# Routing tokens to experts: a row-count sort on chip and narrow column pieces in four pairs, in place of a fixed pairing with an overflow pair

## What is computed

```python
def hierarchical_moe(h, w_rg, b_rg, w_re, b_re, w_gate, w_up, w_down):
    ...
    pg = jax.nn.softmax(g_logits, axis=-1)
    pg_top, g_idx = lax.top_k(pg, 1)
    ...
    pe_top, j_idx = lax.top_k(pe, TOP_K)
    weights = pg_top * pe_top / jnp.sum(pe_top, axis=-1, keepdims=True)
    e_idx = g_idx * EXPERTS_PER_GROUP + j_idx
    combine = jnp.sum(jax.nn.one_hot(e_idx, N_EXPERTS, dtype=jnp.float32) * weights[..., None], axis=1)
    ...
    for e in range(N_EXPERTS):
        act = jax.nn.silu(hf @ w_gate[e]) * (hf @ w_up[e])
        y = y + combine[:, e:e + 1] * (act @ w_down[e])
    return y.reshape(b_, s_, d_)
```

## Time and profile before

| | us |
|---|---|
| three runs | 1675.55, 1676.64, 1677.65 (median 1676.64) |
| the profiled execution, its time | 1675.31 |
| the profiled execution, its span | 1673.4 |
| TensorE busy over the span | 1571.5 |
| VectorE busy | 825.1 |
| ScalarE busy | 543.1 |
| GpSimd busy | 84.3 |

### The profile page before, as it was taken

The page is one execution under the profiler, slowest core; times in us unless marked ns, Lnnn a source line. Parts: engine busy times, 40 slices in busy tenths (PEclk is TensorE's granted clock), DMA queues, the critical chain, the costliest instruction groups (busy, mean ns, idle before and its releaser), DMA issues.

```text
span 1673.4 us, 19707 instructions
## 1 busy us (share of the span) xinstructions
PE 1571.5 (94%) x8009; PEld 1183.4 (71%) x8009; DVE 825.1 (49%) x1442; ACT 543.1 (32%) x881; POOL 84.3 (5%) x106
## 2 busy tenths in 40 slices
PE   7999999999999999999999899999999996888875
PEld 7987777777787788888887688787678883333322
DVE  6546334355355776666323884437663736222211
ACT  5334444354433322222113433342354323111110
POOL 5000000000000000000000010000000001121110
PEclk9999999999999999999999999999999996989998
DMA  5334212122233455565222232221214467999995
GB/s 164 116 101 128 76 51 76 51 76 76 69 95 114 151 183 190 186 221 176 101 101 89 60 103 87 89 66 62 76 51 151 159 231 303 382 414 403 402 407 188
DMA packets 147070, 260.41 MB, mean 156 GB/s; under 512 B 16568, under 2 KB 121316, under 8 KB 133664
## 3 DMA queue, kind: packets, MB, share of 16 engines
q1 hardware_dynamic: 138544, 241.41, 41.1%
q0 software_dynamic: 8432, 17.70, 3.6%
HBM read 253.79 MB, written 15.25 MB: 161 GB/s over the span
## 4 chain that ended last, share of the span: by engine, by line
PE 83%; DVE 7%; issue 4%; ACT 3%; DMA 2%; POOL 0%; POOLq 0%; DVEq 0%; ACTq 0%
PE psum L2498 20%; PE psum L2499 20%; PE psum L2500 20%; PE psum L3079 7%; PE psum L3096 4%; PE psum L2809 1%; PE psum L2798 1%; PE psum L2781 1%; PE psum L3057 1%; DVE cst L2012 1%; DVE WL L1560 1%; DMA Xg<-h_rows,tok 1%; PE psum L2703 1%; ACT Sb L1114 1%; DMA h_rows<-h2t 1%
## 5 line engine op out<-in xcount | busy, mean ns | idle before, releaser
L1560 DVE TENSOR_TENSOR WL<-raw,WH 128x2048 fp32r<-128x2048 f32 (+1 forms) x100 | 226.6, 2266 | 177.1 <-ACT WH L1029 176.8
L2498 PE MATMUL psum<-AHs,WH 128*128 128x512 f32 x744 | 305.9, 411 | 7.5 <-DVE WL L1560 4.6
L2500 PE MATMUL psum<-AHs,WL 128*128 128x512 f32 x744 | 292.6, 393 | 0.0
L2499 PE MATMUL psum<-ALs,WH 128*128 128x512 f32 x744 | 292.1, 393 | 0.0
L1029 ACT ACTIVATE WH<-raw 128x2048 fp32r<-128x2048 f32 (+1 forms) x100 | 189.0, 1890 | 129.1 <-PE psum L2500 97.7
L2498 PEld LDWEIGHTS psum<-AHs,WH 128*128 128x128 f32 x744 | 141.4, 190 | 44.3 <-DVE ALs L1748 5.8
L2498 PE MATMUL psum<-AH,WH 128*128 128x512 f32 (+1 forms) x464 | 169.2, 365 | 0.0
L2499 PE MATMUL psum<-AL,WH 128*128 128x512 f32 (+1 forms) x464 | 164.0, 353 | 0.0
L2499 PEld LDWEIGHTS psum<-ALs,WH 128*128 128x128 f32 x744 | 141.6, 190 | 30.9 <-issue 3.1
L2500 PE MATMUL psum<-AH,WL 128*128 128x512 f32 (+1 forms) x464 | 163.2, 352 | 0.0
L2500 PEld LDWEIGHTS psum<-AHs,WL 128*128 128x128 f32 x744 | 140.9, 189 | 30.7
(11 more groups left out here) (561 smaller groups left out, 2277.4 us busy)
## 6 DMA issues: line engine op xcount, KB each, us to landing
raw<-w_in SPq DMA_DIRECT2D x45, 1024.0 KB, 5.2
WE<-w_gate SPq DMA_DIRECT2D x34, 1024.0 KB, 19.3
WE<-w_up SPq DMA_DIRECT2D x34, 1024.0 KB, 23.1
WE<-w_down SPq DMA_DIRECT2D x34, 1024.0 KB, 19.0
araw<-w_ada SPq DMA_DIRECT2D x24, 1024.0 KB, 5.6
raw<-w_ffn_in SPq DMA_DIRECT2D x22, 1024.0 KB, 7.9
...
```

What stands on the lines that cost most here:

```text
L1560: V.tensor_tensor(WL[:, n, 0:w], raw[:, n, 0:w], WH[:, fed[0] % HL, 0:w].bitcast(F32), ALU.subtract).then_inc(S_("lo_ready"), 1)
L2498: MM(dst, lh, rh, start=first, stop=False)
L2499: MM(dst, lh, rl, start=False, stop=False)
L2500: return MM(dst, ll, rh, start=False, stop=last)
```

## The change

Three experts of each half of the list (13 to 15 and 29 to 31) stay at fixed pairs 0 to 2 (`HELD` = 3), since their weights are loaded before the counts are known. The other 13 of each half are sorted by row count on chip, the first half falling and the second half rising, and fill pairs 3 to 15. Each half of a pair takes 64 rows except in four pairs: in pairs 3 and 4 the first expert has 96 rows and the second 32, in pairs 14 and 15 it is the reverse. A half of 96 rows is worked as a product of 64 and one of 32 stationary columns (`parts_of`), so such a pair issues three products where others issue two. `OVER` is gone, `BASE` is 16; the branch runs if any expert has more rows than its place. SyncE reads both expert numbers of each pair from a list `order` (made by `sorted_places` on VectorE) ahead of its loads. `widths` and `rows_and_pairs` are the rest of the index work on VectorE, which moves behind pair 0's row and gate steps; y_scaled(0) moves behind gated(1).

```diff
-BASE = NE // 2 + 1
-NPAIR = BASE + NOV - 2
-
-OVER = 3
+BASE = NE // 2
+NPAIR = BASE + NOV
+
+HELD = 3
+SORTED = NE // 2 - HELD
+WIDE = 2
...
+        def held(t, half):
+            return NE // 2 * half + SORTED + t
+
+        def parts_of(t):
+
+            if t >= BASE:
+                return [(0, CAP, 0)]
+            if HELD <= t < HELD + WIDE:
+                return [(0, 64, 0), (64, 96, 0), (96, 128, 1)]
+            if t >= BASE - WIDE:
+                return [(0, 32, 0), (32, 64, 1), (64, 128, 1)]
+            return [(0, 64, 0), (64, 128, 1)]
 
         choice_gap, choice_exp, weight1, weight2 = (r4[:, n, :] for n in (0, 1, 2, 3))
 
         def more_tiles(eng):
 
             eng.wait_ge(*when("overflow_ready", 1))
-            return eng.value_load(eover[0:1, NOV:NOV + 1], min_val=0, max_val=NOV) > 2
+            return eng.value_load(eover[0:1, NOV:NOV + 1], min_val=0, max_val=NOV) > 0
 
 
         @block.sync
...
+            load_gate(sp, 2, 1, held(2, 1), 0)
             sp.wait_ge(*when("dense_ready", len(GROUPS)))
-            load_expert(sp, 1, 1, 1)
-            load_gate(sp, 2, 0, 2, 0)
+            load_expert(sp, 1, 1, held(1, 1))
+            load_gate(sp, 2, 0, held(2, 0), 0)
             sp.wait_ge(*when("h2_stored", 16 * NB))
-            load_gate(sp, 2, 1, NE // 2 + 2, 1)
-            sp.wait_ge(*when("overflow_ready", 1))
-            over = [sp.value_load(eover[0:1, x:x + 1], min_val=0, max_val=NE - 1) for x in range(2)]
+            load_gate(sp, 2, 1, held(2, 1), 1)
+            sp.wait_ge(*when("order_ready", 1))
             sp.wait_ge(*when("out_set", 16 * 3))
-            load_pair(sp, OVER, over)
-            for t in range(OVER + 1, BASE):
-                x = t - 1
-                load_pair(sp, t, (x + NE // 2, x) if x % 2 else (x, x + NE // 2))
+            for t in range(HELD, BASE):
+                load_pair(sp, t, [sp.value_load(order[0:1, x:x + 1], min_val=0, max_val=NE - 1)
+                                  for x in (t - HELD, SORTED + t - HELD)])
             with sp.If(more_tiles(sp)):
...
@@ -967,15 +982,9 @@
                     pool.wait_ge(*when(f"y_stored{(t - 1) % 2}", y_stores(t - 1)))
                 else:
                     pool.wait_ge(*when("out_set", 16 * 3))
-                if t == OVER:
-                    pool.wait_ge(*when("tokover_ready", 1))
-                for half in range(2 if t == OVER else 1):
-                    if half:
-                        pool.wait_ge(*when(f"y_stored{t % 2}", y_stores(t) - 16))
-                    rows = tokover[:, half:half + 1] if t == OVER else rows_of_pair(t)
-                    pool.indirect_dma_start(out=out[0], out_offset=bass.IndirectOffsetOnAxis(ap=rows, axis=0),
-                                            in_=Yt[:, t % 2, :], in_offset=None, bounds_check=S - 1, oob_is_err=False,
-                                            compute_op=ALU.add).then_inc(S_(f"y_stored{t % 2}"), 16)
+                pool.indirect_dma_start(out=out[0], out_offset=bass.IndirectOffsetOnAxis(ap=rows_of_pair(t), axis=0),
+                                        in_=Yt[:, t % 2, :], in_offset=None, bounds_check=S - 1, oob_is_err=False,
+                                        compute_op=ALU.add).then_inc(S_(f"y_stored{t % 2}"), 16)
 
             def out_columns(c0, c1):
                 pool.wait_ge(*when("xtm_copied", c1))
@@ -992,8 +1001,9 @@
             gather(0)
             gather(1)
             out_columns(6, KC)
-            pool.wait_ge(*when("over_tokens", 1))
             for t in range(BASE):
+                if t + 2 == HELD:
+                    pool.wait_ge(*when("over_tokens", 1))
                 if t + 2 < BASE:
                     gather(t + 2)
                 scatter(t)
...
-            link(V.tensor_tensor_scan(incl, base_, over, 0.0, ALU.mult, ALU.add))
-            link(V.tensor_tensor(base_, incl, over, ALU.subtract))
             dve.wait_ge(*when("base_used", 1))
-            token_of(tok, 5).then_inc(S_("tokens_ready"), 1)
+            token_of(tok[:, 0:HELD], 5, HELD).then_inc(S_("tokens_ready"), 1)
+
+            sides = [P, 2, SORTED, SORTED]
+
+            def movable(x):
+                return x.rearrange("p (s e) -> p s e", s=2)[:, :, 0:SORTED]
+
+            def sorted_places():
+
+                key = movable(incl)
+                link(V.scalar_tensor_tensor(incl, cnt, float(NE), K("expert"), ALU.mult, ALU.subtract))
+                link(V.tensor_tensor(versus, key.unsqueeze(2).to_broadcast(sides), key.unsqueeze(3).to_broadcast(sides), ALU.is_ge))
+                link(V.tensor_reduce(movable(wider), versus, AX_X, ALU.add))
+                link(V.tensor_scalar(places[:, 1, 0:SORTED], wider[:, 0:SORTED], HELD - 1.0, None, ALU.add))
+                link(V.tensor_scalar(places[:, 1, NE // 2:NE // 2 + SORTED], wider[:, NE // 2:NE // 2 + SORTED], -1.0, float(BASE),
+                                     ALU.mult, ALU.add))
+                link(V.tensor_tensor(versus, movable(places[:, 1, :]).unsqueeze(2).to_broadcast(sides),
+                                     K("expert")[:, HELD:BASE].unsqueeze(1).unsqueeze(3).to_broadcast(sides), ALU.is_equal))
+                link(V.tensor_tensor(versus, versus, movable(K("expert")).unsqueeze(2).to_broadcast(sides), ALU.mult))
+                named = r8[:, 11:15].rearrange("p c n t -> p (c n t)")[:, 0:2 * SORTED]
+                link(V.tensor_reduce(named.rearrange("p (s e) -> p s e", s=2), versus, AX_X, ALU.add))
+                V.tensor_copy(order, named).then_inc(S_("order_ready"), 1)
+
+            def widths():
+
+                link(V.tensor_scalar(wider, places[:, 1, :], HELD - 0.5, None, ALU.is_ge))
+                link(V.scalar_tensor_tensor(wider, places[:, 1, :], HELD + WIDE - 0.5, wider, ALU.is_ge, ALU.subtract))
+                link(V.scalar_tensor_tensor(wider, places[:, 1, :], BASE - WIDE - 0.5, wider, ALU.is_ge, ALU.add))
+                for side in range(2):
+                    half = slice(NE // 2 * side, NE // 2 * side + NE // 2)
+                    link(V.tensor_scalar(cap[:, half], wider[:, half], 64.0 * side - 32.0, float(CAP), ALU.mult, ALU.add))
+                link(V.tensor_tensor(cnt, cnt, cap, ALU.subtract))
+                full_blocks(over, cnt, thr[:, 0, :], steps7[0])
+                link(V.memset(base_, 1.0))
+                link(V.tensor_tensor_scan(incl, base_, over, 0.0, ALU.mult, ALU.add))
+                link(V.tensor_tensor(base_, incl, over, ALU.subtract))
+                for n, x in ((2, places[:, 0, :]), (3, places[:, 1, :]), (4, base_), (7, cap)):
+                    chosen(by_tile[n], x.unsqueeze(1).unsqueeze(1), prod[1])
+
+            def rows_and_pairs():
+
+                link(V.tensor_tensor(rk, rkh, home, ALU.subtract))
...
+                link(V.scalar_tensor_tensor(extra, bs, BASE - 1.0, blk, ALU.add, ALU.add))
+                link(V.tensor_tensor(extra, extra, pair, ALU.subtract))
...
-            link(V.tensor_tensor(pair, pair, w1_, ALU.add))
-            link(V.tensor_scalar(more, more, 1.0, HOME, ALU.is_equal, ALU.mult))
-            link(V.tensor_tensor(more, more, home, ALU.subtract))
...
@@ -2467,15 +2516,20 @@
             def pairs(t0, t1):
                 xt_copy(t0)
                 if t0 == 0:
-                    overflow_numbers()
-                    overflow_tokens()
-                    token_weights()
+                    widths()
                 for t in range(t0, t1):
                     gated(t)
+                    if t == 1:
+                        overflow_tokens()
+                        weights_by_row()
+                        y_scaled(0)
+                        overflow_numbers()
                     if t + 1 < t1:
                         xt_copy(t + 1)
                     if t == 0:
-                        weights_by_row()
+                        rows_and_pairs()
+                        token_weights()
+                        continue
                     y_scaled(t)
 
             pairs(0, BASE)
...
-
-                        rows = slice(CAP * half, CAP * half + CAP)
-                        ins = MM(bank(3)[rows], XT[:, t % 2, P * k + CAP * half:P * k + CAP * half + CAP],
+                    for lo, hi, half in parts_of(t):
+
+                        ins = MM(bank(3)[lo:hi], XT[:, t % 2, P * k + lo:P * k + hi],
                                  GU[gate_up_slot(t, half)].rearrange("p (g k n) -> p k g n", g=2, k=KC)[:, k],
                                  start=k == 0, stop=k == KC - 1)
                 ins.then_inc(S_("gu_done"), 1)
...
-                            rows = slice(CAP * half, CAP * half + CAP)
+                        for lo, hi, half in parts_of(t):
                             o = 2 * DE * KC + D * j + 512 * n
-                            ins = MM(bank(4 + n)[rows], AT[:, t % 2, P * j + CAP * half:P * j + CAP * half + CAP],
+                            ins = MM(bank(4 + n)[lo:hi], AT[:, t % 2, P * j + lo:P * j + hi],
```

(7 more changed lines are left out.)

117 lines of the change are left out of this document (60 added, 57 removed).

## The result

The changed kernel takes 1709.53 us (median of four runs, 1706.97 to 1710.59) against 1677.14 us of the kernel before in the same job (1675.55 to 1679.15). The ratio is 1.0192, with a 95% interval of 1.0176 to 1.0207: slower by 1.9%. (A ratio here compares the runs of one job and isn't exactly the quotient of the two medians.) The forecast was 1697.0 and its range ended at 1703, so the direction and the main mechanism came out as forecast, and the time lies 12.5 us above it. The profiled execution took 1709.28 us, with a span of 1707.5.

What follows compares the result with a forecast made beforehand. TensorE was taken as the bound, loads close behind: gate_up(3) at 1452.4 + 12 x 13.69 + 3 x 13.4 = 1656.9; tail 24.8 + 13.4 gives 1695.1; 1.9 around the span gives 1697.0 us. Whole range 1658 to 1703.

Steps and rivals of the forecast that it cites:

- The wide pairs: Gate_up and down of pairs 3, 4, 14, 15: each width change empties the array, 13.4 us more a pair.
- rival (1): Wide pairs: pieces of 64, 32 and 32 columns run side by side, price 0, time 1659.7 us; chance 0.27.
- (2): Wide pairs: two pieces at a time without a gap, 5.2 us a pair, time 1666.7 us; chance 0.09.
- The tail: From the start of gate_up(15) to the end: 24.8 us plus 13.4 for the wide pair.
- the branch: Overflow branch: does not run, as the row counts fit; if it ran, about 1777 us, chance 0.01.
- What the drain is made of: One chunk of a wide pair: four passes of 0.43 and two changes of 0.13, 1.98 us, 1.12 more.
- Index work: VectorE's lists hide behind gate_up(1), no wait; index products ahead of pair 2's transposes cost TensorE 1.1 us.
- The gather: Rows of pair 3: gather issued at 1436.1, 9.61 us to land, so TensorE waits 1.1 us.
- TensorE stays the bound: Late pairs: weights up to pair 14 there at 1628, TensorE comes at 1629.8, so loads do not bind.
- The reads of `order`: SyncE's two register reads ahead of each pair's loads: cost nothing, 2 us at the other end.
- Rival (3): Whole kernel: the forecast's mechanism with two or three drops of granted clock on top, 1700 to 1706 us; chance 0.07.

Runs made afterwards that it cites:

- experiment 1: Changed kernel with a wide pair's products as four of 32 columns instead of 64, 32 and 32: 1668.11 us, ratio 0.9948 to the kernel before.
- experiment 2: Changed kernel with a wide pair's products grouped by width, all of 64 columns first, then those of 32: 1699.32 us (one execution).
- experiment 8: Kernel before with only its last pair's (16) products as 64, 32 and 32 columns instead of 64 and 64: 1691.20 us, ratio 1.0095.
- Experiment 3: Changed kernel with the gather of pair 3 issued ahead of the scatter of pair 0: 1704.74 us, ratio 1.0161 to the kernel before.
- experiment 6: Changed kernel, widths kept, with the two experts of pairs 5 to 8 changed in place: 1707.34 us, ratio 1.0191 to the kernel before.
- experiment 7: Kernel before without its alternation, so the first half's expert has rows 0 to 63 in every pair: 1679.69 us against 1675.84, ratio 1.0028.
- experiment 5: Experiment 1 with the two experts of pairs 5 to 8 changed in place: 1662.54 us, ratio 0.9925 to the kernel before.
- experiment 10: Experiment 5 with the next pair's expert numbers read ahead of SyncE's wait for the down slots: 1662.37 us, ratio 0.9914 to the kernel before.

## Why the prediction was right and wrong

Of the 12.4 us by which the span was longer than forecast, 4.3 are there by gate_up(5) and 7.1 more by gate_up(14). Two steps failed. The loads were said not to bind, and they did, at pair 13. And the sum had no term for the lowered clock that followed both waits, the gather's and the loads' (2.64 and 2.84 us).

- **The wide pairs: right.** The step that decided the sign was the bound that was taken, each change of width empties the array and unlike widths don't overlap. 13.3 us measured for 13.4. Experiments 1, 2 and 8 show it alone. Rivals (1) and (2), where the pieces run side by side or by twos, fall: no gate_up of 64, 32 and 32 in this order took under 15.9 us, and grouped by width it still took 14. The tail was 38.34 for 38.2, and the branch didn't run (32 loads of each weight).
- **What the drain is made of: half right.** The prediction's word for it was the change of width; the changes are about 2 of 8.9 us. The other 7 are half-filled passes that would have shared the time, two for each chunk. The sum had both, 4 x 0.43 and 2 x 0.13.
- **Index work: right.** TensorE came for the lists at 1430.6 and did not wait; the products cost 0.6 us, not 1.1, and gate_up(2) was 0.6 us earlier than forecast.
- **The gather: under-sized.** "With 9.61 to land" took the shortest of the 14 landings that the trace of before has there (median 10.8); here it was 11.54. The wait was 3.33 us, not 1.1. The step that failed more is that a wait was counted only by its own length: behind it the down took 2.6 us longer at a lowered clock. Experiment 3 gives both back at gate_up(3).
- **"TensorE stays the bound": wrong.** Weights for pair 14 were put at 1628 and TensorE at 1629.8, a margin of 1.8 us on a sum of 120, and pair 13 was not looked at. In fact the loads bound at pair 13 and cost 3.5 us of waiting and 2.84 of clock. Three things ate the margin: the queue refilled 6 us later (5.85 us, of which 4.3 came through the gather and 0.9 from the start), it needed 125 us rather than 120, and the rows stood on one half of the DMA engines (3.3 us at pair 13, experiment 6). The third did little by itself: with the rows shared out the wait stands at pair 14.
- **What the prediction didn't see.** The change also drops a line, left out of the cut of the diff above and shown in experiment 7, that turned the home of every odd expert over. It looked like bookkeeping of the pairs; it kept the rows even over the DMA engines. Experiment 7 prices it at 4 to 5 us in the kernel before, experiment 5 at about 4 in a sorted one without the price of width, and experiment 6 at 1.55 or less with it.
- **The reads of `order`: within the range.** Each pair's two reads delay a gate by 1.2 us. What they cost at the end is 0.2 us by the medians and 1.8 by the ratios of experiments 5 and 10, so the forecast's nothing is neither confirmed nor refuted.
- **Rival (3)** was the forecast with a lower clock on top, 1700 to 1706, at 0.07. That is what came, with late loads besides: 5.5 us of clock in two places. It was sized as two or three drops but given too little of the chance, and the range was cut at 1703 within it. Both drops followed waits of over 3 us, as the row of 9.79 behind 3.79 in the earlier trace rows had done. But a wait doesn't always bring one: the 3.25 us of the same brought none. In the 13 traces 16 gate_ups stand behind a wait of 3 us or more; 10 of them took 1.4 to 2.8 us longer than usual and 6 did not. A forecast that has waits in it should carry their clock as a term with a chance.
- **What the loads are worth: wrong in rival (1).** It put a kernel without the width price at 1659.7, counted for the profiled execution. That of experiment 1 took 1665.07 us and that of experiment 5 1660.55: one pair's loads gone is worth 15.6 us only if the rows don't lean on one side.
